# Gate and up tiles of a feed-forward layer: three 256-wide products in half a PSUM bank instead of a 512-wide and a 256-wide one in a whole bank

## What is computed

```
def rms_norm(x, g):
    y = xf * lax.rsqrt(jnp.mean(xf * xf, axis=-1, keepdims=True) + NORM_EPS)
    return (y * g.astype(jnp.float32)).astype(x.dtype)

def swiglu(h, w_gate, w_up, w_down):
    return (jax.nn.silu(h @ w_gate) * (h @ w_up)) @ w_down

x = x + swiglu(rms_norm(x, ffn_norm[l]), w_gate[l], w_up[l], w_down[l])   # D_FF = 5632, twice
```

## Time and profile before

| | |
|---|---|
| median of 3 runs | 1775.51 us |
| profiled execution | 1775.12 us |
| its span in the profile | 1773.2 us |
| TensorE busy | 1762.1 us, 10370 matmuls |
| VectorE busy | 1133.2 us |
| ScalarE busy | 914.8 us |
| mean rate of the DMA engines | 185 GB/s |

### The profile page before, as it was taken

The page is one execution under the profiler, slowest core; times in us unless marked ns, Lnnn a source line. Parts: engine busy times, 40 slices in busy tenths (PEclk is TensorE's granted clock), DMA queues, the critical chain, the costliest instruction groups (busy, mean ns, idle before and its releaser), DMA issues.

```text
span 1773.2 us, 29180 instructions
## 1 busy us (share of the span) xinstructions
PE 1762.1 (99%) x10370; PEld 1560.7 (88%) x10370; DVE 1133.2 (64%) x1456; ACT 914.8 (52%) x1174; POOL 112.7 (6%) x132
## 2 busy tenths in 40 slices
PE   9999999999999999999999999999999999999998
PEld 5888888888888888889999888888888888888886
DVE  5766666556666666678997776666655566666553
ACT  6666664334444453456775456666533344445433
POOL 2200000000000001123111420000000000000000
PEclk9999999999999999999999999999999999999999
DMA  7555557545555566544445555555655455556642
GB/s 274 198 189 189 189 193 233 185 160 178 189 188 189 189 223 196 175 154 147 158 136 167 190 189 189 189 189 189 226 201 167 165 189 189 189 189 222 227 144 72
DMA packets 85728, 328.78 MB, mean 185 GB/s; under 512 B 9648, under 2 KB 10800, under 8 KB 85552
## 3 DMA queue, kind: packets, MB, share of 16 engines
q1 hardware_dynamic: 85536, 327.09, 55.1%
q10 hardware_dynamic: 144, 1.05, 0.2%
HBM read 326.01 MB, written 2.10 MB: 185 GB/s over the span
## 4 chain that ended last, share of the span: by engine, by line
PE 97%; DVE 2%; ACT 1%; issue 0%; POOL 0%; ACTq 0%; DVEq 0%; POOLq 0%
PE ps L427 57%; PE ps L428 31%; PE ps L497 1%; PE ps L435 1%; PE ps L437 1%; PE ps L436 1%; PE ps L787 1%; PE ps L786 1%; PE ps L788 1%; DVE w_lo L1210 0%; PE ps L623 0%; PE ps L625 0%; PE ps L624 0%; DVE xg L1220 0%; PE ps L677 0%; DVE x L1272 0%
## 5 line engine op out<-in xcount | busy, mean ns | idle before, releaser
L1210 DVE TENSOR_TENSOR w_lo<-raw,w_hi 128x1024 fp32r<-128x1024 f32 (+2 forms) x564 | 736.7, 1309 | 420.6 <-ACT w_hi L831 418.7
L427 PE MATMUL ps<-xg,w_hi 128*128 128x512 f32 x2880 | 999.7, 390 | 0.2 <-DVE w_lo L1210 0.2
L831 ACT ACTIVATE w_hi<-raw 128x1024 fp32r<-128x1024 f32 (+2 forms) x565 | 631.9, 1120 | 552.9 <-PE ps L428 537.1
L428 PE MATMUL ps<-xg,w_lo 128*128 128x256 f32 x2880 | 812.1, 282 | 0.0
L427 PEld LDWEIGHTS ps<-xg,w_hi 128*128 128x128 f32 x2880 | 540.7, 188 | 113.8 <-DVE w_lo L1210 0.6
L428 PEld LDWEIGHTS ps<-xg,w_lo 128*128 128x128 f32 x2880 | 544.3, 189 | 0.1
L427 PE MATMUL ps<-act,w_hi 128*128 128x512 f32 x1320 | 458.0, 390 | 0.0
L428 PE MATMUL ps<-act,w_lo 128*128 128x256 f32 x1320 | 372.2, 282 | 0.0
L427 PEld LDWEIGHTS ps<-act,w_hi 128*128 128x128 f32 x1320 | 247.8, 188 | 51.9
L428 PEld LDWEIGHTS ps<-act,w_lo 128*128 128x128 f32 x1320 | 249.5, 189 | 0.0
L1290 DVE TENSOR_TENSOR sums<-ps,cross 128x512 f32<-128x512 f32 x88 | 60.9, 692 | 95.5 <-ACT cross L908 95.2
(11 more groups left out here) (196 smaller groups left out, 1217.4 us busy)
## 6 DMA issues: line engine op xcount, KB each, us to landing
raw<-w_gate SPq DMA_DIRECT2D x176, 512.0 KB, 3.2
raw<-w_up SPq DMA_DIRECT2D x176, 512.0 KB, 3.2
raw<-w_down SPq DMA_DIRECT2D x120, 704.0 KB, 4.2
raw<-w_o SPq DMA_DIRECT2D x32, 512.0 KB, 3.2
raw<-w_last SPq DMA_DIRECT2D x11, 512.0 KB, 3.2
raw<-w_q_a SPq DMA_DIRECT2D x8, 512.0 KB, 3.2
raw<-w_kv_a SPq DMA_DIRECT2D x8, 512.0 KB, 3.2
raw<-w_q_nope SPq DMA_DIRECT2D x8, 512.0 KB, 3.7
```

The source lines that it names most:

```text
L427: pe.matmul(ps[:, bank, :], w_hi[:, s, j * P:(j + 1) * P], moving, start=start, stop=False)
L428: return pe.matmul(ps[:, bank, 0:SEQ], w_lo[:, s, j * P:(j + 1) * P], moving[:, 0:SEQ], start=False, stop=stop)
L831: nc.scalar.activation(dst, src, ACT.Copy).then_inc(hi_ready, 1)
L1210: nc.vector.tensor_tensor(lo, src, hi.bitcast(F32), ALU.subtract).then_inc(lo_ready, 1)
```

## The change

In the four up stages `product3` becomes `product_one`. The cross copy on ScalarE and the addition on VectorE go; VectorE reads the first halves of the two banks and multiplies by `rstd` in one operation that also frees the banks. Since `sums` may now be written sooner, this operation waits for the Silu of the pair before it. The semaphore `sums_ready` goes, and its one waiter (the Silu) waits for `evacuated` instead.

```diff
-                        mm = product3(n + c, j, (t + m) % 4, xg[:, kt, :], kt == 0, kt == DT - 1)
+                        mm = product_one(n + c, j, (t + m) % 4, xg[:, kt, :], kt == 0, kt == DT - 1)
...
-                        long_tile(n0 + BODY * peel + 2 * f, t0 + 4 * peel + f, xg, TILES, i, 4)
+                        long_tile(n0 + BODY * peel + 2 * f, t0 + 4 * peel + f, xg, TILES, i, 4, product=product_one)
...
-                sc.wait_ge(chunks_used, plus(n + 4, i, BODY))
-                nc.scalar.activation(cross[:, :, :], ps[:, bank:bank + 2, SEQ:], ACT.Copy).then_inc(cross_ready, 1)
                 splits[0]()
-                sc.wait_ge(sums_ready, plus(p * FH + f + 1, i, 2))
+                sc.wait_ge(evacuated, plus(t + 2, i, 4))
                 nc.scalar.activation(gate_act[:, :], sums[:, 0, :], ACT.Silu).then_inc(gate_ready, 1)
...
-                ve.wait_ge(cross_ready, plus(crossed[0] + f + 1, i, 2))
-                nc.vector.tensor_tensor(sums[:, :, :], ps[:, bank:bank + 2, 0:SEQ], cross[:, :, :],
-                                        ALU.add).then_inc(evacuated, 2)
+                ve.wait_ge(chunks_used, plus(n + 4, i, BODY))
+                if p or f:
+                    ve.wait_ge(gate_ready, plus(p * FH + f, i, 2))
+                r = rstd[:, :].rearrange("p (o t) -> p o t", o=1).broadcast_to([P, 2, SEQ])
+                nc.vector.tensor_tensor(sums[:, :, :], ps[:, bank:bank + 2, 0:SEQ], r, ALU.mult).then_inc(evacuated, 2)
+                splits[0]()
                 ve.wait_ge(evacuated, plus(t + 2, i, 4))
-                r = rstd[:, :].rearrange("p (o t) -> p o t", o=1).broadcast_to([P, 2, SEQ])
-                nc.vector.tensor_tensor(sums[:, :, :], sums[:, :, :], r, ALU.mult).then_inc(sums_ready, 1)
-                splits[0]()
```

More of the change, by code:

```diff
@@ L257, in trunk @@
         cross_ready = sem("cross_ready")
-        sums_ready = sem("sums_ready")
         gate_ready = sem("gate_ready")
@@ L555, in ffn @@
                     sum_over_partitions(stats)
-                    long_tile(n0 + 4, t0 + 2, xg, TILES)
-                    long_tile(n0 + 6, t0 + 3, xg, TILES)
+                    long_tile(n0 + 4, t0 + 2, xg, TILES, product=product_one)
+                    long_tile(n0 + 6, t0 + 3, xg, TILES, product=product_one)
                 with pe.Fori(0, FH // 2 - peel) as i:
                     for f in range(4):
-                        long_tile(n0 + BODY * peel + 2 * f, t0 + 4 * peel + f, xg, TILES, i, 4)
+                        long_tile(n0 + BODY * peel + 2 * f, t0 + 4 * peel + f, xg, TILES, i, 4, product=product_one)
                 n0, t0 = CHUNK[DOWNS[p]], TILE[DOWNS[p]]
@@ L904, in ffn_tile @@
                 n, t = CHUNK[UPS[p]] + 4 * f, TILE[UPS[p]] + 2 * f
-                bank = t % 4
-                sc.wait_ge(chunks_used, plus(n + 4, i, BODY))
-                nc.scalar.activation(cross[:, :, :], ps[:, bank:bank + 2, SEQ:], ACT.Copy).then_inc(cross_ready, 1)
                 splits[0]()
-                sc.wait_ge(sums_ready, plus(p * FH + f + 1, i, 2))
+                sc.wait_ge(evacuated, plus(t + 2, i, 4))
                 nc.scalar.activation(gate_act[:, :], sums[:, 0, :], ACT.Silu).then_inc(gate_ready, 1)
@@ L1286, in ffn_tile @@
             def ffn_tile(p, f, splits, i=None):
-                t = TILE[UPS[p]] + 2 * f
+                n, t = CHUNK[UPS[p]] + 4 * f, TILE[UPS[p]] + 2 * f
                 bank = t % 4
-                ve.wait_ge(cross_ready, plus(crossed[0] + f + 1, i, 2))
-                nc.vector.tensor_tensor(sums[:, :, :], ps[:, bank:bank + 2, 0:SEQ], cross[:, :, :],
-                                        ALU.add).then_inc(evacuated, 2)
+                ve.wait_ge(chunks_used, plus(n + 4, i, BODY))
[4 more added lines that the diff above has]
+                splits[0]()
                 ve.wait_ge(evacuated, plus(t + 2, i, 4))
-                r = rstd[:, :].rearrange("p (o t) -> p o t", o=1).broadcast_to([P, 2, SEQ])
-                nc.vector.tensor_tensor(sums[:, :, :], sums[:, :, :], r, ALU.mult).then_inc(sums_ready, 1)
-                splits[0]()
                 ve.wait_ge(gate_ready, plus(p * FH + f + 1, i, 2))
@@ L1331, in ffn @@
                 ffn_tile(p, FH - 1, (nothing, nothing, lambda: split(n0 + 4 * FH - 1 + SPLIT_SLOTS)))
-                crossed[0] += FH
                 n1, t1 = CHUNK[DOWNS[p]], TILE[DOWNS[p]]
```

## The result

The changed kernel takes 1788.81 us (median of 4; 1787.05 to 1789.15), the kernel before 1775.41 us (1775.25 to 1775.96): a ratio of 1.0075, 95% interval 1.0063 to 1.0087. It is slower by 13.4 us. I had forecast slower, by 9.2 us, with a range up to 1787.0; the time lies 1.8 us above it. The profiled execution took 1788.87 us, its span is 1787.0 us: 13.8 us more than before.

A forecast was written before the change was run, and what follows sets the result against it. TensorE's matmul spacing was taken to bound the kernel: 2792 × 3.34 ns = 9.3 us, other terms 0, on 1775.12 gives 1784.4 us profiled; predicted median 1784.6, range 1782.2 to 1787.0.

The forecast's parts named there:

- What bounds the kernel: Up stages: only the spacing of TensorE's own matmuls sets the time; TensorE busy 99%, one 0.2 us wait for `w_lo`.
- What is removed on ScalarE and VectorE: Up stages: 52.6 us of copies and 60.9 us of additions go, beside TensorE, which waits for none; gain 0.
- the added wait: VectorE's `sums` waits for the Silu of the pair before; it would have to come 5 us late to cost; taken as 0.
- The triple dearer than the pair: Each up-stage k-tile: three 256-wide matmuls take 350.0 ns against 346.66 for the pair, +3.34 ns, over 2816 k-tiles 9.4 us.
- The spacing of the triple: Read from 15 periods in the attention's heads before the change: 350.0 ns a k-tile, applied to 2816 k-tiles.
- The bounds of that step: Rounding of starts leaves the triple's spacing known to about 0.7 ns either way, 2.0 us each way on 2816 k-tiles.
- The two rules of the Trainium skill: Up-stage matmuls: issue gap of about 2.5 ns each gives 7.0 us; weight-load busy share says the change uses the last tenth.
- A: Rival: up-stage triple at 349.2 ns, a smaller fixed cost of 2.5 ns a k-tile, 7.0 us: 1782.3; chance 0.07.
- B: Rival: every up-stage matmul costs 13.3 ns on top of its columns, triple 360 ns, +37.5 us: 1812.6; chance 0.03.
- C: Rival: up-stage triple shrinks to 330 ns, priced from a run of six fp32 128-wide matmuls, -47 us: 1728; chance 0.02.
- D: Rival: no change, VectorE's and ScalarE's relief gives back what TensorE loses in the up stages, within 0.2%; chance 0.04.

The follow-up runs named there:

- the pairs with the new chain: Changed kernel with TensorE back on the earlier pairs in all four up stages, ScalarE and VectorE keeping the shortened chain: 1775.17 us against 1775.27, ratio 0.9999.
- the run with `w_lo` in the middle: Changed kernel with the triple ordered w_hi by hi, w_lo by hi, w_hi by lo: 1785.82 to 1786.82 us, median 1786.37.

## Why the prediction was right and where it failed

- What bounds the kernel: right. TensorE's spacing alone, no wait in the up stages, before and after.
- What is removed on ScalarE and VectorE and the added wait, at 0: right, shown by the pairs with the new chain, 0.9999. The relief itself was forecast a little too large, 61 and 53 us where 53.8 and 48.6 were measured: in the earlier trace rows each operation starts about 0.1 us before the one ahead of it ends, and busy time counts such an overlap once.
- The triple dearer than the pair, and the sign: right. The third matmul costs 3.34 ns a k-tile: 4.45 us measured for `up1` and `up3`, 4.7 worked out.
- The spacing of the triple: the step that failed. I took 350.0 ns for all 2816 k-tiles. Half of them ran at 353.34: 672 behind the sum in each of `up0` and `up2`, 1344 × 3.34 = 4.5 us. 9.3 + 4.5 is 13.8, the whole difference of the spans.
- The bounds of that step: for the spacing I called 0.7 ns of rounding the only uncertainty, from a single stretch. The trace of before had the other value. Timeline of TensorE, the first head, where triples start after a wait:

```profile
830.13 0.36 PE L435 MATMUL ps<-latent,w_hi 128*128 128x256 f32 x1 [0.45 <-DVE key_raw L1439]
...
830.56 0.28 PE L435 MATMUL ps<-latent,w_hi 128*128 128x256 f32 x1
...
835.50 0.28 PE L435 MATMUL ps<-latent,w_hi 128*128 128x256 f32 x1
```

There are 14 periods between the last two, 353 ns each; the earlier trace rows are the same code 22 us later at 350. In the changed kernel's profile the same 14 periods, entered after a wait of 0.46 us where it was 0.45, take 4.90 us from 837.64 to 842.54, 350.0 each: the same code took either value. With both ends kept, the range would have run to 1784.6 + 9.4 = 1794 and held the time.
- The two rules of the Trainium skill. The trace disagrees with the 325 and 327.5 ns that the prediction worked out from the Trainium skill (TensorE: Matmul & The Clock Gate, Back-to-back issue gap), and the difference of 2.5 ns was too small in both states: 3.3 and 6.7 ns measured. That section calls its formula the gap of an isolated matmul and says that a stream of weight loads and matmuls follows it neither at small nor at large widths; the prediction left this out. The weight loads are busy the whole of the stretch 60.2 to 280 after, which is where the Trainium skill (Perfetto Trace Analysis, Identifying the Most-Contended Engine) would look for headroom, beside the share of the peak rate that the matmuls reach; but the share cannot tell the two states, as it is full in the fast stretch of the earlier trace rows as well.
- Rivals: A (1782.3) and B (1812.6) had the size of a fixed cost wrong, C had the sign wrong, and D saw no change; none had two states. The six matmuls of the earlier trace rows, on which C's price stands, are transposes of the attention and no product like the triple's.

What stays open: why the stream locks, and what in its entry decides. With the 256-wide fp32 sum directly ahead of the triples, `up2` was slow in all eight profiles of it, `up1` and `up3` in the one that had it, but `up0` in only five of eight. One difference is on record: `up2` runs from its start to the sum at an even 350.0, while in `up0` TensorE waits for a `w_lo` eight k-tiles ahead of the sum, and the length of this wait differs (0.23 us in the changed kernel, 0.18 us in the run with `w_lo` in the middle). That it decides `up0` is likely and was not tested. And the kernel before has a counterexample, in the attention, where two such sums, at 825.49 and 825.92, stand directly ahead of triples: from the L435 at 826.71 to the one at 829.16 there are 7 periods of 350.0 ns. So a lone 256-wide fp32 matmul is neither needed for the slow state (a stall did it) nor always enough. What the engine does in the extra 3.3 ns is not in the trace.

## What to carry to other kernels

Where one engine's spacing is the whole bound, a split of a wide matmul into more narrow ones is paid in each k-tile (here 3.3 ns at the least), and work taken off the others buys nothing. Before a spacing from one stretch is multiplied by thousands, look at every stretch of the same form, above all behind waits and foreign matmuls, and keep the dearest as the end of the range. If such a stream is slower in one stage than in another with no wait, try another matmul, or another width, where it is entered.

## What the runs showed of the hardware

- A steady stream of 256-wide fp32r matmuls, three a k-tile, ran at 350.0 or 353.3 ns a k-tile for 230 us on end, at the same clock. The DMA traffic beside it did not decide which: 353 at 0 and at 190 GB/s, 350 at 189 and at 276; the stream of pairs (512 and 256 wide) ran at 346.7 in all stages, also directly behind the same sum.
- The state changed only at an interruption (a lone fp32 matmul of 256 columns in `up1`, `up2` and `up3`, or a stall of 1.7 us), never within the 670 k-tiles that follow in a stage, in any profile. With one more matmul behind the sum it came out fast: -3.9 us of time.
- Two matmuls with the same weights in a row cost as much as with another matmul between them: 350.0 and 353.3 ns a k-tile in both orders.
